# VectorE in place of GpSimd for the low halves of the weight slabs, at the end of its work on each slab

## What is computed

```
for i in range(DEPTH):
    h = rmsnorm(x, norm_mix[i])
    if i % 2 == 0:
        u, v, z, xbc, dt_raw = jnp.split(h @ l0_w_in, SPLIT0, axis=-1)
        ya, gm_v = gmlp_mix(u, v, ...)
        yb, ... = mamba_mix(z, xbc, dt_raw, ...)
        x = x + jnp.concatenate([ya, yb], axis=-1) @ l0_w_out
    else:
        x = x + retention_mix(h, ...)
    h = rmsnorm(x, norm_ffn[i])
    x = x + conv_ffn(h, ...)                # (silu(conv(h @ w_gate)) * (h @ w_up)) @ w_down
    gate = jax.nn.sigmoid(rmsnorm(x, norm_ple[i]) @ ple_w_gate[i])
    x = x + gate * (p[i] @ ple_w_proj[i])
x = rmsnorm(x, norm_final)
```

## Time and profile before

| what | us |
|---|---|
| median of 3 runs | 1858.17 (1857.85 to 1858.92) |
| profiled execution | 1858.24 |
| its span in the trace | 1856.5 |
| busy, TensorE matmuls | 1816.7 |
| busy, VectorE | 955.9 |
| busy, ScalarE | 622.5 |
| busy, GpSimd | 847.5, of which 652.3 are the 276 low halves of weights |
| loads of weights | 512 KB a slab, 3.4 from issue to landing (median) |

### The profile page before, as it was taken

The page is one execution under the profiler, slowest core; times in us unless marked ns, Lnnn a source line. Parts: engine busy times, 40 slices in busy tenths (PEclk is TensorE's granted clock), DMA queues, the critical chain, the costliest instruction groups (busy, mean ns, idle before and its releaser), DMA issues.

```text
span 1856.5 us, 34451 instructions
## 1 busy us (share of the span) xinstructions
PE 1816.7 (98%) x14145; PEld 1768.9 (95%) x14145; DVE 955.9 (51%) x1547; ACT 622.5 (34%) x896; POOL 847.5 (46%) x415
## 2 busy tenths in 40 slices
PE   8999999999999999999899999999999999999996
PEld 7999988999999999999899999999899999999995
DVE  6456777565533542556644441344555415515554
ACT  5334423343221222244433332233334313212342
POOL 4333423466544544565533334333365545544662
PEclk9999999999999999999999999999999999999998
DMA  6222201222342232223222222222122222222221
GB/s 231 79 73 69 80 23 35 74 86 80 114 138 89 81 103 90 74 79 98 80 77 77 77 76 80 88 77 78 54 91 82 89 90 90 91 92 82 66 93 48
DMA packets 49475, 156.80 MB, mean 84 GB/s; under 512 B 5984, under 2 KB 10208, under 8 KB 49376
## 3 DMA queue, kind: packets, MB, share of 16 engines
q1 hardware_dynamic: 43776, 147.67, 24.4%
q10 hardware_dynamic: 5600, 7.74, 1.3%
HBM read 149.75 MB, written 5.63 MB: 84 GB/s over the span
## 4 chain that ended last, share of the span: by engine, by line
PE 90%; DVE 6%; ACT 2%; issue 1%; POOL 0%; DMA 0%; DVEq 0%; POOLq 0%; ACTq 0%
PE proj L318 81%; PE Q L925 6%; DVE arena L1753 1%; ACT arena L622 1%; DVE op_lo L389 1%; DVE arena L1616 0%; DVE arena L1606 0%; ACT op_hi L376 0%; PE Q L1202 0%; DVE rstd L369 0%; DVE x L1755 0%; DVE ssq L1426 0%; PE proj L925 0%; DVE arena L1393 0%; PE Q L329 0%
## 5 line engine op out<-in xcount | busy, mean ns | idle before, releaser
L414 POOL TENSOR_TENSOR w_lo<-w_raw,w_hi 128x1024 fp32r<-128x1024 f32 (+2 forms) x276 | 652.3, 2364 | 760.0 <-ACT w_hi L340 759.7
L318 PE MATMUL proj<-op_hi,w_hi 128*128 128x256 f32 (+1 forms) x4272 | 895.6, 291 | 9.5 <-DVE op_lo L389 5.7
L318 PE MATMUL proj<-op_hi,w_lo 128*128 128x256 f32 (+1 forms) x4272 | 884.6, 288 | 0.0
L318 PE MATMUL proj<-op_lo,w_hi 128*128 128x256 f32 (+1 forms) x4272 | 877.8, 287 | 0.0
L318 PEld LDWEIGHTS proj<-op_hi,w_hi 128*128 128x128 f32 x4272 | 683.5, 189 | 22.6 <-issue 12.3
L318 PEld LDWEIGHTS proj<-op_lo,w_hi 128*128 128x128 f32 x4272 | 686.3, 189 | 0.0
L318 PEld LDWEIGHTS proj<-op_hi,w_lo 128*128 128x128 f32 x4272 | 682.0, 188 | 0.0
L340 ACT ACTIVATE w_hi<-w_raw 128x1024 fp32r<-128x1024 f32 (+2 forms) x276 | 284.8, 1032 | 651.0 <-PE proj L318 650.0
L1393 DVE TENSOR_TENSOR arena<-proj,rstd 128x512 f32<-128x512 f32 (+1 forms) x143 | 98.7, 690 | 220.9 <-PE proj L318 195.4
L1400 DVE TENSOR_TENSOR x<-proj,x 128x512 f32<-128x512 f32 x72 | 49.7, 690 | 223.2 <-PE proj L318 223.2
L622 ACT ACTIVATE arena<-arena 128x32 f32<-128x32 f32 (+5 forms) x217 | 106.0, 514 | 54.6 <-DVE arena L1606 33.2
(11 more groups left out here) (171 smaller groups left out, 1040.2 us busy)
## 6 DMA issues: line engine op xcount, KB each, us to landing
w_raw<-in_w_gu SPq DMA_DIRECT2D x88, 512.0 KB, 3.4
w_raw<-in_w_down SPq DMA_DIRECT2D x32, 512.0 KB, 3.4
w_raw<-in_w_heads_a SPq DMA_DIRECT2D x30, 512.0 KB, 3.4
w_raw<-in_w_heads_b SPq DMA_DIRECT2D x18, 512.0 KB, 3.4
w_raw<-in_w_gate SPq DMA_DIRECT2D x16, 512.0 KB, 3.4
w_raw<-in_w_xbc SPq DMA_DIRECT2D x12, 512.0 KB, 3.3
w_raw<-in_w_down SPq DMA_DIRECT2D x16, 384.0 KB, 3.0
w_raw<-in_w_v SPq DMA_DIRECT2D x8, 512.0 KB, 8.2
```

The source lines that it names most:

```text
L318: last = nc.tensor.matmul(proj[:, 2 * g.mod(2) + half, 0:size], w[:, lo:lo + P], o[:, at:at + size], start=(k == 0 and j == 0), stop=(k == ...
L414: nc.gpsimd.tensor_tensor(w_lo[:, c:c + width], w_raw[:, c:c + width], w_hi[:, c:c + width], ALU.subtract).then_inc(w_lo_done, 1)
```

## The change

The low half of slab n+4 is made by VectorE, as the last thing that it does for slab n, in every phase. The first four slabs, which are made before any phase begins, stay with GpSimd, and VectorE waits once (w_lo_done at 4) before its first. The subtraction is the same instruction with the same operands and the same wait for w_hi_done, and it raises the same semaphore. 272 of the 276 low halves change engine (four of gate1's eight slabs have none to make: no slab follows). GpSimd keeps its other work. `with_lows` wraps a phase's body on VectorE; it uses `each_ahead`, which writes a phase out without a loop where slab widths change. Line numbers of unchanged code move a little: L1393 and L1396 become L1379 and L1382, L1400 and L1401 become L1386 and L1387, L1577 becomes L1573, L1594, L1606 and L1616 become L1592, L1604 and L1614, L560, L588 and L604 become L552, L576 and L592.

```diff
--- before.py
+++ after.py
@@ -406,18 +406,19 @@
-        def split_low(pool, s):
+        def split_low(eng, issue, s):
 
             width = phase_of(s.c).width
             c = s.mod(RING) * SLAB
-            pool.wait_ge(w_hi_done, (s + 1).v)
-            nc.gpsimd.tensor_tensor(w_lo[:, c:c + width], w_raw[:, c:c + width], w_hi[:, c:c + width],
-                                    ALU.subtract).then_inc(w_lo_done, 1)
-
-        def low_ahead(pool, ph, n):
-            s = n + (ph.s0 + RING)
+            eng.wait_ge(w_hi_done, (s + 1).v)
+            issue(w_lo[:, c:c + width], w_raw[:, c:c + width], w_hi[:, c:c + width], ALU.subtract)\
+                .then_inc(w_lo_done, 1)
+
+        def low_ahead(dve, name, n):
+            n = n if isinstance(n, At) else At(n)
+            s = n + (PH[name].s0 + RING)
             if n.k or s.c < NSLABS:
-                split_low(pool, s)
+                split_low(dve, nc.vector.tensor_tensor, s)
...
             for n in range(RING):
-                split_low(pool, At(n))
+                split_low(pool, nc.gpsimd.tensor_tensor, At(n))
...
             for p in range(NC + 1):
                 chunk(p, TS if p == 0 else CH)
-                for n in SSD_MIXED[p] + SSD_END[p]:
-                    low_ahead(pool, PH["outa"], At(n))
...
+            def with_lows(name, body, peel=0):
+                def one(n):
+                    body(n)
+                    low_ahead(dve, name, n)
+                each_ahead(dve, PH[name], one, 4, peel)
...
+                if n == 0:
+                    dve.wait_ge(w_lo_done, RING)
+                low_ahead(dve, "v", n)
...
             add_to_x(group("outa", 0), At(0))
+            low_ahead(dve, "outa", 0)
...
                 for n in SSD_END[p]:
                     add_to_x(group("outa", n), At(n))
+                for n in SSD_MIXED[p] + SSD_END[p]:
+                    low_ahead(dve, "outa", n)
...
-            each(dve, KD, z_body)
+            with_lows("z", z_body)
...
-                        each(dve, KD, last_down)
+                        with_lows(down, last_down)
...
-                each(dve, 4, pp_body)
+                with_lows(f"pp{layer}", pp_body)
...
-                each(dve, KD, gate_body)
+                with_lows(f"gate{layer}", gate_body)
```

More of the change, by code:

```diff
@@ L533, in _, with phase @@
             sub, mul = ALU.subtract, ALU.mult
-            def phase(name, job=None, per=4):
-                def one(n):
-                    low_ahead(pool, PH[name], n)
-                    if job:
-                        job(n)
-                each_ahead(pool, PH[name], one, per)
+            def phase(name, job):
+                each(pool, PH[name].slabs, job)
             pool_squares(pool, "n_in", None)
             for n in range(RING):
-                split_low(pool, At(n))
+                split_low(pool, nc.gpsimd.tensor_tensor, At(n))
             pool.wait_ge(sem("wdt_hi"), 1)
             nc.gpsimd.tensor_tensor(w_dt_lo[:, :], w_dt[:, :], w_dt_hi[:, :], sub).then_inc(sem("wdt_lo"), 1)
-            phase("v")
-            phase("u")
-            phase("xbc")
-            low_ahead(pool, PH["outa"], At(0))
             def chunk(p, rows):
@@ L589, in head @@
                                     .then_inc(sem("r_sin"), 1)
-                    heads(pool, head, lambda: phase("ret_a"))
+                    heads(pool, head, lambda: None)
                     pool_squares(pool, "n_ffn1", "n_mix1")
@@ L609, in _ @@
                         phase(f"down{layer}2", lambda n: pool_square(pool, PLE[layer], n))
-                    else:
-                        phase(f"down{layer}{part_}")
                     off += nt
-                phase(f"pp{layer}")
                 nxt = ("n_mix1", "n_out")[layer]
@@ L1258, in _, with retention_dve @@
             mean_square(pe, "n_out")
-        def retention_dve(dve, scaled, add_to_x, group):
+        def retention_dve(dve, scaled, add_to_x, group, with_lows):
             add, sub, mul = ALU.add, ALU.subtract, ALU.mult
@@ L1375, in drain @@
                 turn5(At(7), At(6))
-            heads(dve, head, lambda: each(dve, KD, lambda n: add_to_x(group("ret_a", n), n)), drain)
+            heads(dve, head, lambda: with_lows("ret_a", lambda n: add_to_x(group("ret_a", n), n)), drain)
             def last(n):
@@ L1380, in last @@
                 dve_operand(dve, "n_ffn1", n, part(x, n, 0, T))
-            each(dve, KD, last)
+            with_lows("ret_b", last)
         @block.vector
@@ L1556, in _ @@
                     ya_low(n - U_FIRST - 1)
+                low_ahead(dve, "u", n)
             for q in range(2):
@@ L1580, in _ @@
                     ya_low(late + n - 1)
+                low_ahead(dve, "xbc", n)
             add_to_x(group("outa", 0), At(0))
+            low_ahead(dve, "outa", 0)
             dve.wait_ge(sem("decays"), 1)
@@ L1672, in outb_body @@
                 dve_operand(dve, "n_ffn0", n, part(x, n, 0, T))
-            each(dve, KD, outb_body)
+            with_lows("outb", outb_body)
             for layer in range(2):
                 if layer:
-                    retention_dve(dve, scaled, add_to_x, group)
+                    retention_dve(dve, scaled, add_to_x, group, with_lows)
                     dve.wait_ge(sem("ret_stored"), 1 + 32 * RH)
@@ L1721, in gate_up @@
                                 .then_inc(sem("f_lo"), 1)
-                    each(dve, 2 * nt, gate_up, peel=0 if off or layer else 4)
+                    with_lows(gu, gate_up, peel=0 if off or layer else 4)
                     down = f"down{layer}{part_}"
                     if part_ < 2:
-                        each(dve, KD, lambda n: add_to_x(group(down, n), n))
+                        with_lows(down, lambda n: add_to_x(group(down, n), n))
                     else:
```

3 lines of the change are left out of this document (1 added, 2 removed).

## The result

| | us |
|---|---|
| before, median of 9 runs | 1858.23 (1857.85 to 1859.60) |
| changed, median of 9 runs | 1863.16 (1860.44 to 1865.71) |
| ratio, with its 95% interval | 1.0026 (1.0016 to 1.0036) |
| profiled execution of the changed kernel | 1860.83, span 1859.0, granted clock 0.991 |

The changed kernel is slower by a quarter of a percent. 1860.5 was forecast with a range of 1855.0 to 1864.5, so the median lies in the range, 2.7 us above the forecast. It also lies 1.3 us above the bound that I had set between "no difference" (0.60) and "slower" (0.26): the case that I held for likeliest is not the one that came. And the runs are more than three times as far apart as those of before, 5.3 us against 1.75, which no part of the prediction speaks of.

The account below looks back on a forecast made before the run. TensorE, busy 98% of the span, was taken as the bound, so only places where its chain of waits runs through VectorE count: +1.7 +3.2 -1.6 -1.0 = +2.3 us on 1858.24, giving 1860.5 us, range 1855.0 to 1864.5.

Parts of the forecast that it names:

- no difference: Whole kernel: time from 1854.45 to 1861.9 us, not to be told from before; chance 0.60.
- slower: Whole kernel: time over 1861.9 us; chance 0.26.
- Who holds whom: VectorE and GpSimd, two-input SBUF work: not side by side; GpSimd, having asked during VectorE's instruction, goes before VectorE's next.
- Rival (b): pp: VectorE becomes the bound once a low half costs over 1.38 us start to start; 1863.8 us, chance 0.15.
- Gate0, +1.7: First gate phase: low half held by GpSimd's ssq addition, L1753 freed; net +0.30 us a slab, sum +1.7 us.
- the ring: Gate0: VectorE and ScalarE's turns for one slab, forecast at 6.8 us against TensorE's 6.
- the longest wait of 6 to 7 us: Before the heads: TensorE's longest wait, 5.2 us before the change, was to become 6 to 7 us.
- Down to pp, +3.2: Last down phase to projection phase: held low half delays VectorE's copy by 1.6 us in each of two layers.
- rival (a): VectorE keeps its turn: the queued low half goes ahead of GpSimd's ssq; sum -8.0, 1850.2 us, chance 0.12.
- Chunks, -1.6: State-space chunks: entry -1.5 us, boundary of chunks 0 and 1 -0.3, of 2 and 3 +0.2; together -1.6.
- End of z, -1.0: End of the z phase: L1663 falls to 0.72 us, operand and ssq end 1.7 earlier, TensorE gains 1.0 us.
- The rest, at nothing: FFN, chunk bodies, heads and ret phases: low halves stay hidden behind TensorE's work, 0 us.

Follow-up runs that it names:

- after_look1: The changed kernel run again without any edit, to profile one of its longer executions; that execution took 1862.93 us.
- after_look2: The changed kernel run once more without any edit, again to profile a longer execution; that execution took 1863.79 us.
- pool_chunks2: The changed kernel with the 8 low halves made in outa, between xbc and z, back on GpSimd: 1861.77 us (10 runs).
- Low_before_op: The changed kernel with the low half ahead of L389 in z, outb, ret_b, the last down phases and gate0: 1848.88 us, ratio to before 0.9945.
- double_low2: The changed kernel with each low half made twice in most FFN phases and in heads_a, ret_a and heads_b (116 more instructions): 1875.22 us.
- pool_gate0: The changed kernel with the 8 low halves made in gate0 back on GpSimd: 1861.25 us (10 runs).

## Why the prediction was right and wrong

**Who holds whom: right.** GpSimd's addition, issued inside L389, goes first; the low half behind it ended at 1.09 us behind GpSimd's end, the very number of the sum, and 1.22 us where nothing held it against the 1.23 taken from L1594. Rival (b), a dearer low half, is out by the same rows. The about 115 ns that the Trainium skill (SBUF — State Buffer, A bandwidth-pool intuition that's wrong) would add behind the holder's end are not in these rows. (Nine handovers at 115 ns would be 1.0 us, where the prediction has 0.9.)

**Gate0, +1.7: right in the chain, and partly given back behind it.** From the first L1753 (854.14 before, 853.90 now) to the last L389 (902.53 before, 903.96 now) VectorE's chain grew by 1.67 us; the ring is 6.82 as forecast. It arrived on TensorE: from pp0 4 to the last six matmuls of heads_a 1 (903.37 before, 904.80 now) the change loses 1.75 us. By heads_a 3 only 0.9 is left. The difference is in the 1.2 GHz stretch behind the wait, which was there before as well: it ended at 909.1 before and at 908.5 now, so it covers 5.7 us of TensorE's time behind the wait before and 3.7 now, and 2.0 us less at half speed are worth about 1.0. That was no part of the forecast, and it is luck: it hangs on where the slow stretch ends. Of the signs, the longest wait of 6 to 7 us did not come (5.1), since TensorE was already held up twice inside gate0, where the prediction had it never wait.

**Down to pp, +3.2: the step that failed.** The wait was right: 2.04 us where about 2.0 was said, +1.6 in each layer. The term was made of that wait alone. It measured 3.5 in each layer, 7.0 in all: 1.6 the wait, 1.5 TensorE at 1.2 GHz behind it, 0.4 the fourth slab. (The 1.5 came behind 12 of the 14 such waits that were profiled, so in some executions the change is spared it.) The profile of before had shown the second part at another place: I had counted 1.0 us for it in rival (a), behind the 5.2 us wait, and had not asked whether my own new wait of 2 us would bring another. The third part I put at 0 with 2.9 against 3.08 us a slab. That compares rates. With two PSUM tiles the copy of a group must follow its end at once, and a low half that starts late, since ScalarE's high half is late, stands just there.

**Chunks, -1.6: the entry right, a later boundary wrong.** Between outa 1 and outa 3 after_look1 and after_look2 gain 1.7 us on before, with the clock down as there, where I had 1.5. Pool_chunks2 gains 0.4, so 1.3 of it comes with outa's low halves. In the first profile, with the clock up, the gain is 3.9. The boundary of chunks 0 and 1 gave 0.25 of the 0.3 that was forecast. The boundary of chunks 2 and 3 was given +0.2 and cost 1.15, and the one before it 0.4, in every profile of the change. Two low halves stand there ahead of the product of the chunk, which GpSimd then holds:

```profile
285.47 2.35 DVE L414 TENSOR_TENSOR w_lo<-w_raw,w_hi 128x1024 fp32r<-128x1024 f32 x2
287.74 2.93 DVE L1592 TENSOR_TENSOR arena<-arena 128x1024 f32<-128x1024 f32 x1
```

```profile
287.44 2.15 POOL L552 TENSOR_TENSOR arena<-arena,head_rows 128x1024 f32<-128x1024 f32 x1 [18.48 <-ACT arena L607]
```

The product ends 5.1 us behind the addition to x ahead of them, 3.3 in before, and TensorE's longest wait from 255 to 310 us is 2.4 for what follows it, where before had 0.8. I had weighed only who gets in ahead, and not the 2.35 us themselves. pool_chunks2 doesn't have this loss.

**End of z, -1.0: wrong.** It came to nothing. VectorE and GpSimd near z's end (two views):

```profile
380.45 2.39 DVE L414 TENSOR_TENSOR w_lo<-w_raw,w_hi 128x1024 fp32r<-128x1024 f32 x1
...
382.76 0.68 DVE L1379 TENSOR_TENSOR arena<-proj,rstd 128x512 f32<-128x512 f32 x1
...
386.64 0.52 PE L318 MATMUL proj<-op_hi,w_hi 128*128 128x256 f32 x2 [0.78 <-DVE op_lo L389]
```

```profile
380.34 1.41 POOL L405 TENSOR_TENSOR ssq<-ssq,sq 128x544 f32<-128x544 f32 x1 [4.64 <-ACT sq L384]
```

TensorE had finished the tile at about 380.6 (ScalarE's high half starts at 380.65), and VectorE read it at 382.76. The held low half makes z a ring of VectorE of 6.06 us, so the reading runs 2.1 us behind, and this eats the 1.7 that L1663 gave. I had put the low half's end at 0.3 behind the next tile, without the addition that holds it: the mechanism that I had used for gate0 holds in every phase that makes an operand, and I had applied it in two. Low_before_op, where the low half is not held, gains 1.3 us here.

**The rest, at nothing: nearly.** It gave 2.9 us: each of the six gate-and-up phases hands over 0.2 to 0.4 us earlier, and its last L1720 takes 0.73 us in place of 1.08, with no w_lo beside it; the heads and ret phases give 0.7, the phases up to xbc 0.4. There was no new wait, as forecast (TensorE's list of waits from 910 to 1300 us is empty), and double_low2 shows how thin that was in the heads. One row was misread here without harm: 0.97 from 900 to 1000 us is no clock level, but the mean over a slow stretch until 909.1 and full speed behind it.

**The sum.** For the profiled execution the terms were +1.7 +3.2 -1.6 -1.0 = +2.3, and +2.6 was measured (1858.24 to 1860.83). That is luck in good part. By the starts of slabs pp has 3.8 more than its term and z 1.2; against them stand the rest with -2.9, the chunks with -1.0 (the clock stayed up in this execution) and gate0 with -0.8. The median, 2.3 us above that execution, is the middle one of executions that differ, as far as the profiles show, by whether it does. (The chances of the prediction's cases also add up to 0.98 and not to 1.)

## What to carry to other kernels

When work moves to an engine that shares something with the one it leaves, look not at the load but at the instruction just before it: here one instruction up or down was worth 14 us of 1860 (by the medians), with the same work on the same engine. The good place was inside a wait that the engine had anyway (VectorE waiting for ScalarE), and before the other engine's request. Price a new pause of TensorE with the slowed matmuls behind it where the trace shows such a stretch behind another pause, and test a "hidden" by doubling the hidden thing: VectorE busy 54% of the time had some 0.7 us to spare at one place in each head, and 80% in the FFN cost nothing.

## What the runs showed of the hardware

- A pause of TensorE of 2.03 to 2.04 us in an otherwise full stretch was followed by 3.4 us at the 1.2 GHz level in 12 of 14 cases, which began 0.2 to 1.1 us after the pause's end: in both layers of the four profiles of the change and of pool_gate0, in pp1 only of pool_chunks2, in pp0 only of double_low2. It cost 1.5 us each time (4.6 us for a slab in place of 3.08). The 12 pauses of 0.28 to 0.89 us that the other profiles have at the same two places were not followed by one.
- The same program can have TensorE at 1.2 or at 2.4 GHz at one place from one execution to the next (226.5 to 231.0: 0.50 and 1.00), worth 2.2 us, while no other start of a slab moved by 0.15 us. The change's runs spread over 5.3 us where those of before spread over 1.75, and over 2.0 with outa's eight low halves back on GpSimd; that the whole spread comes from such stretches is inferred.
- A VectorE instruction with two inputs in SBUF that was issued while a GpSimd instruction with two such inputs ran ended 1.06 to 1.07 ns per column behind GpSimd's end (1024 columns: 1.09 us; 512: 0.55), where the whole instruction takes 1.22 us for 1024 columns when nothing holds it. So the held one is 0.13 us shorter, counted from GpSimd's end, than a free one.
